# Group 16 of the input projection in seven products: a two-layer hybrid encoder trunk on one core

## The reference

```python
for l in range(DEPTH):                       # 2 layers
    h = _rmsnorm(x, norm_gain[l])
    proj = jnp.einsum('bsd,de->bse', h, w_in[l])          # 2048 -> 4352
    q, k, v, g_attn, x_rnn, g_rnn = jnp.split(proj, splits, axis=-1)
    attn = _swa_sink_attention(q, k, v, sinks[l], cos, sin)
    xc = _causal_conv(x_rnn, conv_w[l], conv_b[l])
    rnn = _rg_lru(xc, ...)
    mixed = jnp.concatenate([attn * jax.nn.silu(g_attn), rnn * jax.nn.silu(g_rnn)], axis=-1)
    x = x + jnp.einsum('bse,ed->bsd', mixed, w_out[l])    # 2048 -> 2048
return _rmsnorm(x, final_gain)
```

## Time and profile before

| | us |
|---|---|
| median of three runs | 2287.01 |
| the profiled execution | 2284.59 |
| its span, first to last instruction | 2282.6 |
| PE busy | 2275.4 |
| DVE busy | 1568.4 |
| ACT busy | 1313.8 |
| POOL busy | 84.5 |

### The profile page before, as it was taken

The page is one execution under the profiler, slowest core; times in us unless marked ns, Lnnn a source line. Parts: engine busy times, 40 slices in busy tenths (PEclk is TensorE's granted clock), DMA queues, the critical chain, the costliest instruction groups (busy, mean ns, idle before and its releaser), DMA issues.

```text
span 2282.6 us, 38226 instructions
## 1 busy us (share of the span) xinstructions
PE 2275.4 (100%) x14446; PEld 1938.9 (85%) x14446; DVE 1568.4 (69%) x2594; ACT 1313.8 (58%) x2536; POOL 84.5 (4%) x138
## 2 busy tenths in 40 slices
PE   9999999999999999999999999999999999999998
PEld 7888888899888888889988888888988888888898
DVE  7658768656546876865677777786568468778555
ACT  7558676444446867645665575664455557566444
POOL 1110000000111000000010000000001100000000
PEclk9999999999999999999999999999999999999999
DMA  8988677445798677645576566675548746666444
GB/s 258 253 234 267 236 240 240 152 137 141 212 235 222 236 235 240 215 113 166 138 226 171 151 201 203 213 235 174 142 129 255 199 135 196 209 202 196 140 134 153
DMA packets 175575, 447.01 MB, mean 196 GB/s; under 512 B 21024, under 2 KB 25376, under 8 KB 170528
## 3 DMA queue, kind: packets, MB, share of 16 engines
q1 hardware_dynamic: 168048, 381.56, 53.2%
q0 software_dynamic: 6912, 62.92, 11.7%
q10 hardware_dynamic: 432, 0.10, 0.0%
HBM read 365.85 MB, written 141.56 MB: 222 GB/s over the span
## 4 chain that ended last, share of the span: by engine, by line
PE 98%; DVE 1%; DMA 1%; ACT 0%; issue 0%; POOL 0%; DVEq 0%; ACTq 0%; POOLq 0%
PE proj L720 74%; PE proj L741 18%; PE ps_at L849 2%; PE ps_at L824 1%; PE ps_at L868 1%; PE proj L760 1%; DMA wall<-in_w 1%; PE proj L787 0%; ACT wcut L943 0%; DVE mixed L1829 0%; PE ps_at L675 0%; DVE acc L1440 0%; ACT operand L980 0%; PE ps_at L802 0%; ACT sqr L1006 0%
## 5 line engine op out<-in xcount | busy, mean ns | idle before, releaser
L720 PE MATMUL proj<-operand,wcut 128*128 128x512 f32 x7512 | 1745.6, 391 | 0.0
L720 PEld LDWEIGHTS proj<-operand,wcut 128*128 128x128 f32 x7512 | 1399.8, 188 | 298.0 <-issue 9.3
L1345 DVE TENSOR_TENSOR wcut<-wall,wcut 128x512 fp32r<-128x512 f32 x799 | 550.2, 689 | 536.8 <-ACT wcut L943 530.7
L943 ACT ACTIVATE wcut<-wall 128x512 fp32r<-128x512 f32 x798 | 501.7, 629 | 592.3 <-DMA wall<-in_w 319.8
L741 PEld LDWEIGHTS proj<-operand,wcut 128*128 128x128 f32 x1476 | 187.8, 191 | 6.4
L741 PE MATMUL proj<-operand,wcut 128*128 128x256 f32 x1476 | 189.8, 283 | 0.0
L741 PE MATMUL proj<-xsum_out,wcut 128*128 128x256 f32 x1104 | 136.8, 283 | 0.0
L741 PEld LDWEIGHTS proj<-xsum_out,wcut 128*128 128x128 f32 x1104 | 134.9, 192 | 0.6
L741 PE MATMUL proj<-xsum_in,wcut 128*128 128x256 f32 x864 | 111.8, 284 | 0.0
L741 PEld LDWEIGHTS proj<-xsum_in,wcut 128*128 128x128 f32 x864 | 107.9, 191 | 3.5 <-issue 1.7
L1049 ACT ACTIVATE gy<-proj 32x512 f32<-32x512 f32 x144 | 85.0, 590 | 13.1 <-PE proj L720 7.3
(11 more groups left out here) (186 smaller groups left out, 1732.8 us busy)
## 6 DMA issues: line engine op xcount, KB each, us to landing
wall<-in_w SPq DMA_DIRECT2D x494, 256.0 KB, 2.8
weight_cuts<-wcut SPq DMA_DIRECT2D x126, 512.0 KB, 3.9
wcut<-weight_cuts SPq DMA_DIRECT2D x126, 512.0 KB, 4.1
weight_sums<-in_blocks POOLq DMA_DIRECT2D x84, 512.0 KB, 6.3
wall<-weight_sums SPq DMA_DIRECT2D x164, 256.0 KB, 2.8
wall<-in_blocks SPq DMA_DIRECT2D x141, 256.0 KB, 2.9
weight_sums<-weight_sums POOLq DMA_DIRECT2D x28, 512.0 KB, 4.7
x<-in_xt SPq DMA_DIRECT2D x16, 512.0 KB, 4.1
```

The source lines that it names most:

```text
L720: last = pe.matmul(bank_of(l, 2 * g + m)[:, :], wcut[:, n % RING, a, c:c + P], operand[:, k, b, :], start=(i == 0 and k == 0), stop=(k == ...
L943: act.activation(wcut[:, u % RING, 0, :], wall[:, u % RING, 1, :], ACT.Copy).then_inc(w_hi, 1)
L1345: dve.tensor_tensor(wcut[:, u % RING, 1, :], wall[:, u % RING, 1, :], wcut[:, u % RING, 0, :].bitcast(F32), ALU.subtract).then_inc(w_lo, 1)
```

## The change

`IN_LAST` becomes 16: in half 1 of both layers group 16 is in seven products too. `PARTS` keeps group 16 of half 0 in eight plain units; of these the four that half 1 still uses as plain units are stored split (`KEYS`), so that half 1 loads them ready-made, while the three blocks and the four sums of group 16 are split on the chip. The batches of sums that held group 15 alone now hold groups 15 and 16. `OPENS` has one entry less: the batch for groups 9 and 10 of layer 1 no longer starts at slot 128 of half 1, layer 0, but with those after it at slot 9 of layer 1. The residual comes back tile by tile, with a semaphore for each tile, in half 0 from slot 127 and in half 1 from slot 135.

```diff
--- before.py
+++ after.py
@@ -63,7 +63,8 @@
 STREAM += [(g, j) for g in range(2, PG + OG) for j in range(UPG)]
 X_EARLY = 8
 WARM = 9
-IN_LAST = 15
+IN_LAST = 16
+PARTS = 16
 IN_SEVEN = {(0, 0): (), (0, 1): (), (1, 0): range(7, IN_LAST + 1), (1, 1): range(7, IN_LAST + 1)}
 SEVEN = {(h, l): (*IN_SEVEN[h, l], *range(PG + 2, PG + (7 if (h, l) == (LAST, DEPTH - 1) else 8)))
          for h in range(HALVES) for l in range(DEPTH)}
@@ -88,7 +89,7 @@
 def beats_of(h, l, g):
 
     mine, ahead = g in SEVEN[h, l], g + 1 in SEVEN[h, l]
-    blocks = g in BUILT[l] and zone_of(g) == "in"
+    blocks = g in BUILT[l] and g < PARTS
     p = [("plain", g, j) for j in range(UPG) if not (mine or blocks) or j not in JS[zone_of(g)]]
     a = [("lead", g + 1, b) for b in range(4)]
     t = [("late", g, b) for b in range(3)]
@@ -169,7 +170,8 @@
 KEYS = []
 CUT_AT = {}
 for n, (h, l, kind, g, j) in enumerate(UNIT):
-    if h == 0 and zone_of(g) == "in" and g in BUILT[l] and (kind, j) != ("block", WHOLE[A21]):
+    if h == 0 and g < PG and g in BUILT[l] and (kind == "plain" and j not in JS["in"] or
+                                             kind == "block" and j != WHOLE[A21]):
         CUT_AT[key_of(l, kind, g, j)] = n
         KEYS.append(key_of(l, kind, g, j))
 READY = {n for n, (h, l, *unit) in enumerate(UNIT) if h > 0 and key_of(l, *unit) in CUT_AT}
@@ -223,9 +225,9 @@
 HI_PART = {"in": (0, 0, 0, 1), "out": (0, 0, 0, 0)}
 SPILL = (1, 3, 0, 2)
 SPILL_AT = 1
-RELOAD = UPG * IN_LAST + 7
+RELOAD = (UPG * (PG - 2) + 7, UPG * IN_LAST + 7)
 START_SUMS = 8
-OPENS = {5: (0, 1, 1), 10: (1, 0, 4), 12: (1, 0, 128), 13: (1, 1, 9)}
+OPENS = {5: (0, 1, 1), 10: (1, 0, 4), 12: (1, 1, 9)}
 XQ = 166
 LATE = 5
 XS = O0 + (OG - 1) * UPG + 1
@@ -329,7 +331,7 @@
         par_in = sem("par_in")
         idn_in = sem("idn_in")
         x_in = [sem(f"x_in{i}") for i in range(KT // 2 + 1)]
-        xres_in = [sem(f"xres_in{i}") for i in range(KT // 2)]
+        xres_in = [sem(f"xres_in{i}") for i in range(KT)]
         tab_in = sem("tab_in")
         gw_in = [sem(f"gw_in{i}") for i in range(GRING)]
         built = {n: sem(f"built{n}") for n in SUMS}
@@ -555,21 +557,19 @@
                             sp_.dma_start(x_kept[i, :, 2 * two * TOK:2 * two * TOK + 2 * TOK],
                                           x[:, 4 * i + 2 * two:4 * i + 2 * two + 2, :].rearrange("p k t -> p (k t)")
                                           ).then_inc(kept[i], 16)
-                        for i in range(KT // 2):
-                            if (h, l) in X_BACK and s == RELOAD + 2 * i:
+                        for k in range(KT):
+                            if (h, l) in X_BACK and s == RELOAD[h] + k:
 
                                 if (h, l, "in") in ZONES:
                                     sp_.wait_ge(unit_done, TURNED[h, l, "in"])
                                 if l == 0:
                                     if h > 0:
-                                        sp_.wait_ge(stored[i // 2], 64 * h)
-                                    sp_.dma_start(x[:, 2 * i:2 * i + 2, :], xt[h, :, 2 * i:2 * i + 2, :]
-                                                  ).then_inc(xres_in[i], 16)
+                                        sp_.wait_ge(stored[k // 4], 64 * h)
+                                    sp_.dma_start(x[:, k, :], xt[h, :, k, :]).then_inc(xres_in[k], 16)
                                 else:
-                                    sp_.wait_ge(kept[i // 2], 32 * sum(at < (h, l) for at in X_BACK if at[1] == 1) + 32)
-                                    half = i % 2 * 2 * TOK
-                                    sp_.dma_start(x[:, 2 * i:2 * i + 2, :].rearrange("p k t -> p (k t)"),
-                                                  x_kept[i // 2, :, half:half + 2 * TOK]).then_inc(xres_in[i], 16)
+                                    sp_.wait_ge(kept[k // 4], 32 * sum(at < (h, l) for at in X_BACK if at[1] == 1) + 32)
+                                    part = k % 4 * TOK
+                                    sp_.dma_start(x[:, k, :], x_kept[k // 4, :, part:part + TOK]).then_inc(xres_in[k], 16)
                         for k in range(KT):
                             if h > 0 and l == 0 and s == NS + 2 * k + 2:
 
@@ -1649,8 +1649,8 @@
                 dve.tensor_copy(hlast[:, l, j:j + 1], mixed[:, AT + j, TOK - 1:TOK])
 
             def residual(h, l, t):
-                if t % 2 == 0 and (h, l) in X_BACK:
-                    dve.wait_ge(xres_in[t // 2], 16 * X_BACK.index((h, l)) + 16)
+                if (h, l) in X_BACK:
+                    dve.wait_ge(xres_in[t], 16 * X_BACK.index((h, l)) + 16)
                 group_done(h, l, tile_of("o", t))
                 dve.tensor_tensor(x[:, t, :], bank_of(l, tile_of("o", t))[:, :], x[:, t, :], ALU.add).then_inc(evac, 1)
```

## The result

The changed kernel is slower: 2290.80 us (median of 15 runs, 2287.63 to 2294.92) against 2285.94 us (15 runs of the kernel before beside them, 2284.91 to 2288.01), ratio 1.0018 with a 95% interval of 1.0012 to 1.0025. That is 4.1 us by the ratio (2.7 to 5.7 us by its interval; the medians lie 4.9 us apart). It is at the edge of the 0.2% that I had called no change, yet with 15 runs on either side the interval does not reach 1. The profiled execution took 2287.63 us, span 2285.7 us; it is the fastest of the 15.

What follows compares the result with a forecast made beforehand. PE was taken as the bound, busy 2275.4 of 2282.6 us. Each layer -0.78 us for products and +1.65 for a wait gives +0.87, two +1.74: 2288.75 us from the median, range 2284.5 to 2292.0.

Steps and rivals of the forecast that it cites:

- What PE gains: Half 1, each layer: seven half units replace four plain ones, saving PE 0.78 us after changeovers, 1.56 us in all.
- Where DVE is, and the wait: Ahead of group 17's second unit in half 1, DVE's weight split comes late; PE waits some 1.7 us each layer.
- Rival 1: DVE keeps up ahead of group 17, so PE gains its 1.56 us: 2285.45 us; chance 0.27.
- What is hidden: ACT's work, group 16's transfers, POOL's batches, the residual and SP's further issues and stores were to cost PE nothing.
- the sentence on POOL: Two batches of sums double in size, but end by 1853 us, before their sums are wanted; no cost.
- Rival 2: The first late unit's block of group 16 lands late, 9.8 us, costing 6.3 us in one layer: 2295.0 us; chance 0.10.
- Residual, SP, opening of the batches: Residual tiles load in time, SP's eight more issues and stores fit, moving POOL's batch from slot 128 wins nothing.
- The number: Whole kernel: one wait a layer gives +1.74 us, bounds +0.2 to +3.0, 2288.75 us; chance 0.58.

Runs made afterwards that it cites:

- the two cures: Changed kernel with either the first operand sum at slot 124 in half 1 (ratio 1.0002) or the mixed tiles split one slot later (0.9997).
- the batches spread: Changed kernel with batches of sums moved to stretches of whole units, plus first operand sum at slot 124 (ratio 0.9996) or mixed tiles one slot later (0.9995).
- the operand sum early: Changed kernel with the first operand sum for the output projection at slot 124 instead of 126 in half 1; 2287.15 us, ratio 1.0002.
- the tiles later: Changed kernel with each pair of mixed tiles split one slot later, the last two staying; 2286.12 us, ratio 0.9997.
- one more instruction: Changed kernel with an unused DVE subtraction of 128x512 added at slot 131 of half 1 in each layer; 2290.80 us, ratio 1.0012.
- the old opening: Changed kernel with the batch for groups 9 and 10 of layer 1 back at slot 128 of half 1, layer 0; 2290.95 us, ratio 1.0014.
- the residual alone: Kernel before with only the residual loaded tile by tile from slot 127 in both halves; 2286.30 us, ratio 0.9996.
- both edits: Changed kernel with first operand sum at slot 124 in half 1 and layer 1's batch for groups 7 and 8 at its slot 9; 2286.00 us, ratio 0.9997.

## Why the prediction was right, and where it was not

- *What PE gains*: 0.78 us a layer forecast, 0.76 measured. Right.
- *Where DVE is, and the wait*: from `lead_half_sum` to the end of the second unit's split I had 2077.37 to 2103.47, 26.1 us; measured 1516.78 to 1542.72, 25.9, and as much in layer 1. The wait: 1.65 us forecast, 1.55 measured, at the unit named, in both layers; the first unit was to be just in time, and is, with 0.2 us. Two different edits of DVE's order each take it away, a third makes it longer by nearly its own length: this cause is shown.
- *Rival 1* (DVE keeps up) is out. It is what the two cures make of the kernel, and half 1 then has the gain: 1.5 and 1.7 us in the traces with the batches spread. The whole times do not show it.
- *What is hidden*, the sentence on POOL: this step failed. I costed the doubled batches at nothing, with an argument on when their sums are wanted (right: nothing waited for a sum) and none on what they do to other transfers where they run. The doubled batch of layer 0 starts at 1160 us; from there to 1221 us DVE was busy for 86% of the time in the kernel before, ACT for 64%. In the changed kernel's trace a block ordered near 1196 took 9.5 us to land, and the chain runs from it through ACT and DVE to PE's wait at 1212 (start, us, what):

```profile
1195.95 9.49 DMA wall<-in_w
...
1205.52 0.64 ACT wcut L943
...
1208.65 0.68 ACT mixed L1080
...
1209.88 0.70 DVE wcut L1345
...
1211.09 0.69 DVE gy L1474
1211.78 0.61 DVE gy L1477
...
1212.43 3.69 PE proj L720 x15
```

Blocks ordered from 1195 to 1206 us, from order to landing (least, median, most), in the kernel before, in the changed one and in the one with the batches spread and the operand sum early:

```profile
DMA to landing us min/median/max: 2.8/4.6/5.9
DMA to landing us min/median/max: 5.1/7.3/9.5
DMA to landing us min/median/max: 2.6/2.8/3.0
```

All five traces with the doubled batch and its neighbour there have a wait of PE from 1210 to 1220 us, and in each the chain comes from a late block: the one above, and these, with the operand sum early, the tiles later, one more instruction and the old opening.

```profile
1199.87 11.68 DMA wall<-in_w
1203.34 9.69 DMA wall<-in_w
1196.47 10.07 DMA wall<-in_w
1196.31 13.03 DMA wall<-in_w
```

The waits are 0.6 us for the landing of 9.49, and 2.8, 0.8, 1.2 and 4.0 us for these four in turn: past some 8.9 us, each us of landing was a us of PE's. (Elsewhere the cover differs: in the trace of the residual alone a block ordered at 1188 took 9.4 us and cost nothing.) The two traces with the small batch (the kernel before, the residual alone) have no such wait, nor have the six with the doubled batch or its neighbour moved away, at that place; one of the six, with both edits, has 0.4 and 0.7 us at 1181 and 1183 instead. So late blocks beside these two batches are the cause of the wait near 1212. How much of the median's loss they are is not shown. The mean of the five, 1.9 us, and the half clock behind one of them (below) are about what the median lacked: -1.52 + 3.09 + 1.9 is 3.5 us, for 4.1 us by the ratio. But one trace a kernel is few for a wait that varies so, and the whole times can't tell it: either cure alone has 1.0002 and 0.9997, with batches moved as well it is 0.9997, 0.9996 and 0.9995.
- *Rival 2* (a late block) named the right kind of thing at the wrong place: a late block of group 16 held PE up in none of these traces, late blocks beside the sums did.
- *Residual, SP, opening of the batches*: hidden, as forecast. The residual alone and the old opening both show no difference, and in the changed kernel's trace neither SP waits for a sum nor DVE for the residual. SP's further stores were not tried alone.
- *The number*: the time lies in the range, but the forecast was +1.74 us with bounds of +0.2 to +3.0, and the measured +4.1 lies above them, though its interval, from 2.7, does not wholly. That 2290.80 us lies only 2.05 us over the forecast time has luck in it: the forecast started from a median of three runs, 2287.01 us, and 15 runs put the kernel before at 2285.94.

What stays open is whether the version with the batches spread is faster than the kernel before: its intervals reach 1.0004 and 1.0005, and the waits of half 0 and the last store scatter by as much as the 1.5 us in question.

## What to carry to other kernels

Where one engine is the bound without a gap, making it faster in one stretch takes time from every engine that feeds it there: walk the feeder's list from the last thing it waited for to the first thing that is due, in the trace of before. Here the new wait came out to a tenth of a microsecond. Move an instruction into the feeder's idle time ahead of the walk, or behind the due one, before taking the gain. And cost a background transfer by what runs beside it, not only by when its result is wanted: the cover of a prefetch is a count of units, so it shrinks with their length.

## What the runs showed of the hardware

A wait of PE can cost more than its length. In the trace with the operand sum early, PE waited 2.8 us up to 1218.6, and the granted clock was then 0.50 (1.2 GHz) for 3.4 us, 1.7 us more. The window columns are PE, PEld, DVE, ACT and POOL busy, the clock, DMA share and GB/s:

```profile
1212.00:1218.60 6.60, 4.00 (x19) 2.96 (x17) 4.34 (x8) 6.36 (x11) 0.80 (x1) 1.00 0.99 302
1218.90:1222.20 3.30, 3.30 (x9) 2.58 (x8) 3.17 (x6) 3.17 (x6) 0.52 (x1) 0.50 0.52 124
1222.30:1230.00 7.70, 7.70 (x35) 6.38 (x34) 7.42 (x13) 3.20 (x5) 0.78 (x1) 1.00 0.76 170
```

A wait of 2.2 us at 163 in the trace with the tiles later had the same behind it; waits of 2.7 us at 168 in the former and 2.8 us at 1216 with the old opening had not. The Trainium skill, "TensorE: Matmul & The Clock Gate", section "Why this matters for your kernels", advises against long idle gaps of PE between bursts of matmuls, since the clock drops behind one. The traces agree for two of these waits, though they are only 2.2 and 2.8 us long; the other two, as long, cost only themselves, and what set them apart is open.
